# Where the first group's x tiles live, and what the second group's loads wait for, in a hybrid encoder block

## The reference, cut

```
h = rms_norm(x, g_mix); u = h @ w_in + b_in           # GLU value | gate | q | k | v
y_conv = silu(layer_norm(depthwise_conv31(a * sigmoid(gate))))
y_attn = windowed attention (|i-j| <= 128), 8 q heads, 2 kv heads, rotary, sink logit
x += concat(y_conv, y_attn) @ w_out + b_out
x += cross attention (4 heads) from rms_norm(x) into rms_norm(mem), 256 rows
x += (silu(h @ w_gate) * (h @ w_up)) @ w_down         # h = rms_norm(x), width 2816
out = rms_norm(x, g_final)
```

## Time and profile before

| | |
|---|---|
| timed runs | 2018.51 us median of 3 (2016.75 to 2023.31) |
| profiled execution | 2009.25 us, span of its slowest core (2) 2008.0 us |
| spans of the cores | 1985.2 to 2008.0 us |
| mean granted clock | 0.952 to 0.961 |
| busy | PE 1846.9 us (92%), DVE 1109.5 (55%), ACT 873.2 (43%), POOL 120.6 (6%) |
| chain that ended last | PE 78%, DMA 7%, DVE 5%, issue 5%, SP's queue 3%, ACT 2% |

### The profile page before, as it was taken

One profiled execution on the slowest core, in us unless ns is written; L12 is line 12 of the kernel. 1 busy time (PEld: TensorE's weight loads), 2 busy tenths in 40 slices (PEclk: granted clock), 3 DMA queues, 4 the chain that ended last, 5 costly groups with the idle time before them and its releaser, 6 DMA issues.

```text
span 2008.0 us, 34383 instructions; the slowest of 8 cores (1985.2 to 2008.0 us)
## 1 busy us (share of the span) xinstructions
PE 1846.9 (92%) x11516; PEld 974.5 (49%) x11516; DVE 1109.5 (55%) x2430; ACT 873.2 (43%) x1761; POOL 120.6 (6%) x206
## 2 busy tenths in 40 slices
PE   4989998863389999999999999999999999999997
PEld 2545557741135444544454455445444544544443
DVE  5657666553257546643854485467447644754442
ACT  4535534531155444544545354544445453545210
POOL 2100100000100000000000000000001000000000
PEclk7999998766699999999999999999999999999999
DMA  8898865789763316322622363163326223431542
GB/s 263 209 198 217 176 165 168 148 180 194 124 94 127 124 38 235 114 92 79 231 96 93 124 208 116 46 217 119 103 79 219 97 90 132 168 103 56 188 142 100
DMA packets 80934, 284.71 MB, mean 142 GB/s; under 512 B 7159, under 2 KB 38777, under 8 KB 62872
## 3 DMA queue, kind: packets, MB, share of 16 engines
q1 hardware_dynamic: 73592, 237.74, 37.0%
q0 software_dynamic: 2560, 27.99, 10.6%
q10 hardware_dynamic: 4608, 16.78, 2.0%
HBM read 273.16 MB, written 65.10 MB: 168 GB/s over the span
## 4 chain that ended last, share of the span: by engine, by line
PE 78%; DMA 7%; DVE 5%; issue 5%; SPq 3%; ACT 2%; DVEq 0%; ACTq 0%; POOL 0%; POOLq 0%
PE bank L369 52%; PE bank L1447 15%; PE bank L377 5%; DMA arena<-s_y 3%; SPq L359 3%; PE bank L778 2%; PE bank L1086 2%; DMA s_v<-arena 1%; DMA arena<-w_in 1%; PE bank L512 1%; ACT arena L390 1%; PE bank L1090 1%; DVE arena L1368 1%; DVE arena L1056 1%; DVE arena L1211 0%
## 5 line engine op out<-in xcount | busy, mean ns | idle before, releaser
L369 PE MATMUL bank<-arena 128*128 128x512 bf16 (+1 forms) x5724 | 1274.7, 375 | 13.3 <-DVE stat L394 6.6
L369 PEld LDWEIGHTS bank<-arena 128*128 128x128 bf16 x5724 | 555.1, 98 | 616.0 <-issue 38.8
L1447 PE MATMUL bank<-arena 128*128 128x512 bf16 x1408 | 323.2, 379 | 0.6 <-DVE arena L1458 0.6
L390 ACT ACTIVATE arena<-arena 128x1024 bf16<-128x1024 f32 x130 | 137.2, 1055 | 298.5 <-DVE arena L1458 148.6
L377 PE MATMUL bank<-ident,arena 128*128 128x128 bf16 x2080 | 158.1, 224 | 85.3 <-DVE arena L1211 27.2
L1120 ACT ACTIVATE arena<-bank,asm 128x384 bf16<-128x384 f32 (+1 forms) x256 | 146.8, 573 | 145.1 <-DVE asm L1108 128.8
L1447 PEld LDWEIGHTS bank<-arena 128*128 128x128 bf16 x1408 | 133.7, 98 | 149.6 <-issue 7.5
L1413 ACT ACTIVATE arena<-bank 128x512 f32<-128x512 f32 x176 | 105.3, 598 | 229.5 <-PE bank L369 229.0
L377 PEld LDWEIGHTS bank<-ident,arena 128*128 128x128 bf16 x2080 | 137.3, 100 | 130.4 <-issue 98.3
L1104 DVE TENSOR_REDUCE asm<-bank 128x1 f32<-128x384 f32 (+1 forms) x256 | 139.2, 544 | 64.1 <-PE bank L1090 55.0
L1211 DVE TENSOR_TENSOR arena<-bank,arena 128x512 f32<-128x512 f32 x128 | 88.3, 690 | 153.7 <-PE bank L369 122.1
(11 more groups left out here) (85 smaller groups left out, 1292.9 us busy)
## 6 DMA issues: line engine op xcount, KB each, us to landing
arena<-s_gu SPq DMA_DIRECT2D x88, 1024.0 KB, 4.9
arena<-x SPq DMA_DIRECT2D x64, 512.0 KB, 9.2
arena<-s_wd SPq DMA_DIRECT2D x32, 1024.0 KB, 5.0
out<-arena ACTq DMA_DIRECT2D x32, 512.0 KB, 4.0
arena<-s_wd SPq DMA_DIRECT2D x16, 768.0 KB, 4.2
s_gu<-w_gate_up POOLq DMA_DIRECT2D x11, 1024.0 KB, 13.5
s_mem<-w_memory POOLq DMA_DIRECT2D x8, 1024.0 KB, 13.4
arena<-s_mem SPq DMA_DIRECT2D x8, 1024.0 KB, 8.3
```

The source lines that it names most:

```text
L369: ins = nc.tensor.matmul(out_ap, l, r, start=(k == 0), stop=(k == n - 1))
L390: sc.op("act", lambda: nc.scalar.activation(junk, src, AF.Square, accum_out=st[:, 0:1]), reads=[srcb], writes=[junkb, stb], cost=1.26)
L1447: sc.op("pe", lambda t=t, bk=bk: nc.tensor.matmul(bk[:], actT[c][:, t * P:(t + 1) * P], w3[:, c - c0, :], start=(c == 0), stop=(c == NFC - ...
```

## The change

The x tiles of even groups move from 105 to 56 in the arena, those of odd groups from 56 to 105. A list `gate` gets the second matmul group of the output projection of group 0, tile 0. The loads of q, k, v, y and x of group 1 and the first four FFN weight loads wait for it; the y loads of group 1 get 40 us of slack (the first two at once; tiles 2 and 3 are issued by `ln_z` of tiles 0 and 1, as before). The four weight loads waited for the load of `WO` and the last y load of group 0 before. `pace` is called after the projection instead of before it, in `out_proj` and in `s_mm`, so that the cast waits for that projection.

```diff
-    xres = [[mk((105, 56)[s_] + 4 * t, 4, F32, D) for t in range(4)] for s_ in range(2)]
+    xres = [[mk((56, 105)[s_] + 4 * t, 4, F32, D) for t in range(4)] for s_ in range(2)]
...
-            dma("sp", qT.rearrange("p a n -> p (a n)"), s_q[g], [q_g[g]], [qT_b], qT_sem, (), 0.0 if g else 30.0)
+            dma("sp", qT.rearrange("p a n -> p (a n)"), s_q[g], [q_g[g]], [qT_b], qT_sem, gate if g == 1 else (), 0.0 if g else 30.0)
...
+    gate = []
+
     def pace(g):
         if g == 0:
             next_cast([sc.ops[-1]])
...
-        yl_last[0] = dma("sp", ybuf(g, t)[0], s_y[b * P:(b + 1) * P, :], y_b0 + (y_b1 if g else []), [ybuf(g, t)[1]], yt_sem[t % 2 + (2 if g == 0 and t > 1 else 0)])
+        yl_last[0] = dma("sp", ybuf(g, t)[0], s_y[b * P:(b + 1) * P, :], y_b0 + (y_b1 if g else []), [ybuf(g, t)[1]], yt_sem[t % 2 + (2 if g == 0 and t > 1 else 0)], gate if g == 1 else (), 40.0 if g == 1 else 0.0)
...
-                dma("sp", xs[t][0], x_d[b * P:(b + 1) * P, :], [], [xs[t][1]], xres_sem[g % 2][t])
+                dma("sp", xs[t][0], x_d[b * P:(b + 1) * P, :], [], [xs[t][1]], xres_sem[g % 2][t], gate if g == 1 else ())
...
             def a():
+                st["b"] = proj(t, WO, [WO_b], lambda k: ymixT[:, k, t * P:(t + 1) * P], ymc_b + [yma_b[t]], True)
+                if g == 0 and t == 0:
+                    gate.append(sc.ops[-1])
                 pace(g)
-                st["b"] = proj(t, WO, [WO_b], lambda k: ymixT[:, k, t * P:(t + 1) * P], ymc_b + [yma_b[t]], True)
...
             def s_mm():
+                st["s"] = proj(t, WK, WK_b, lambda k: ha[:, k, :], [hb], False)
                 pace(g)
-                st["s"] = proj(t, WK, WK_b, lambda k: ha[:, k, :], [hb], False)
...
     for j in range(NSLOT):
-        ring_load(j, [wo_op, yl_last[0]])
+        ring_load(j, gate)
```

More of the change, by code:

```diff
@@ L965, in f @@
         def f():
-            dma("sp", qT.rearrange("p a n -> p (a n)"), s_q[g], [q_g[g]], [qT_b], qT_sem, (), 0.0 if g else 30.0)
+            dma("sp", qT.rearrange("p a n -> p (a n)"), s_q[g], [q_g[g]], [qT_b], qT_sem, gate if g == 1 else (), 0.0 if g else 30.0)
             gs = sorted(set(b_ // 4 for b_ in range(b0, b1)))
-            dma("sp", kz[:, :, (b0 - lo) * P:(b1 - lo) * P], s_k[:, :, b0 * P:b1 * P], [k_g[k] for k in gs], [kz_b], kz_sem, (), 0.0 if g else 30.0)
-            dma("sp", vz[:, b0 - lo:b1 - lo, :], s_vv[:, b0:b1, :], [vv_g[k] for k in gs], [vz_b], vz_sem, (), 0.0 if g else 30.0)
+            dma("sp", kz[:, :, (b0 - lo) * P:(b1 - lo) * P], s_k[:, :, b0 * P:b1 * P], [k_g[k] for k in gs], [kz_b], kz_sem, gate if g == 1 else (), 0.0 if g else 30.0)
+            dma("sp", vz[:, b0 - lo:b1 - lo, :], s_vv[:, b0:b1, :], [vv_g[k] for k in gs], [vz_b], vz_sem, gate if g == 1 else (), 0.0 if g else 30.0)
             for t in range(2 if g else 4):
```

## The result

The changed kernel takes **2038.49 us** (median of four), the kernel before 2020.91 beside it: a ratio of 1.0085, 95% interval 1.0064 to 1.0105. That is slower by under 1% but clear of the noise, 17.6 us by the medians, where 2016.5 was forecast, and 2.5 us outside the range. One of the four was a slow run, with half of the cores at a lower clock (2320.09 us; the others took 2036.48, 2037.88 and 2039.11), and all ratios, and the medians of the experiments, leave such runs out, while the only profile of the third kernel of number 6 is of one. The profiled execution took 2036.48 us (span of its slowest core, 3: 2035.2 us), 27.2 us more than that of before. It lies 2.0 us under its median, that of before 9.3 us under the median taken with it (2018.51), so the traces show more of a difference than the medians.

What follows compares the result with a forecast made beforehand. TensorE's own work after about 588 us sets the end, so the first group's FFN start counts. Gains -11, -27.1 and -12.3 make -50.4, gated loads give back +48: -2 us, 2016.5 us from 2018.5; 8-in-10 range 1984 to 2036.

Steps and rivals of the forecast that it cites:

- The case forecast: Second group's LayerNorm step ahead of VectorE's last first-group steps, which wait for y: FFN at 593.6, +5.8 us.
- some 9 us to go: VectorE's last first-group steps behind the second group's LayerNorm step, from y's landing to the FFN start: some 9 us.
- G: The gate, end of output projection 0: 485.6 us before, about 474.6 after.
- (b): Second group's first x loads leave SP's queue ahead of the first y loads: y lands 11 us sooner, bounds 0 and 15.5.
- The gated loads: Second group's loads and four FFN weight tiles behind G, among casts: k at G + 71, y at G + 110; +48 us.
- the other order: LayerNorm step behind VectorE's last first-group steps: TensorE waits for k until G + 71; FFN start worth 577.6, -10.2 us.
- (a): First group's x tiles in the region free first: the 27.1 us x wait goes, less what is late next.
- (c): Mixer casts hung on the projection itself, one projection later: taken at 0, between -2 and +3 us.
- The slower rival: Second group's LayerNorm steps and output projections late, first group's FFN covers only part: 2032.5 us, chance 0.20.
- Full and half relief: Full: gated loads in time, 50.4 us stay, 1968 us, chance 0.15; half: two packets for one, 2001.5 us, chance 0.20.
- The middle: FFN start taken between the two places of the LayerNorm step, +5.8 and -10.2: -2 us; forecast's chance 0.45.

Runs made afterwards that it cites:

- the third kernel of number 6: Kernel before with only its nine late casts issued by first-group FFN units 0, 4, 8, 11, 13, 15, 17, 19 and 21: 1978.37 us, ratio 0.9818.
- Experiment 9: Five casts during and after the convolution issued by its first five steps: in the changed kernel 2025.36 us (1.0067), in the best version so far 1972.09 us (0.9799).
- Experiment 7: Changed kernel with 70 instead of 40 us of planner's slack on the second group's first two y loads: 2024.41 us, ratio 1.0045.
- experiment 4: Changed kernel with the second group's x loads free of the gate: a single execution, 2028.7 us.
- the first kernel of experiment 5: Changed kernel with its nine late casts issued by first-group FFN units 0, 2 to 16 instead of the mixers, every gate kept: 2006.99 us, ratio 0.9957.
- experiment 1: Kernel before with only the two x regions exchanged, no gate, casts as before: 2015.11 us, ratio 0.9992.
- experiment 8: Changed kernel with `pace` ahead of the projections again, gates and regions of the change kept: 2033.43 us, ratio 1.0105.

## Why the prediction was wrong

The case forecast is what happened: VectorE reaches the second group's LayerNorm step ahead of its last steps for the first group and waits there until y lands. With that order the prediction had the FFN at 593.6, 5.8 us later than before; it is at 614.0. The 20.4 us between are three terms. The step of the prediction that failed most is the last one, the "some 9 us to go" for the work behind the LayerNorm step: it measured 25.2.

| term | forecast | measured | us |
|---|---|---|---|
| G | 474.6 | 483.6 | +9.0 |
| y of the second group | G + 110 | G + 105 | -4.8 |
| work left behind the LayerNorm step | 9 | 614.0 - 588.8 = 25.2 | +16.2 |

**(b), the first y: mis-sized, and its row half read.** 11 us sooner was forecast. From the end of the convolution to the first LayerNorm step it was 46.4 us before (415.6 to 462.0 on the profiled core) and is 40.6 now, 6 us less; a y load takes 26.1 instead of 33.2 us, 7 less. So 5 of the 9 us are that; 3.5 more are the convolution's own end, 419.1 instead of 415.6, which differs from core to core by more than that (406.8 to 420.4 in the changed kernel). Over the eight cores the median of G is 481.7 against 482.9 before: 1 us sooner where 11 were forecast. The 141 GB/s of the step came from the row of SP's queue in 426 to 462 us. The same answer has a second row, which the prediction left out:

```profile
q0 software_dynamic: 96, 2.10, 49.3%
```

Two casts held half the DMA time there. In the changed kernel they still do (96 packets, 2.10 MB, 49.2%): three x loads fewer do not free that half. Experiment 9 shows it: without the casts the same loads land in 9.7 us. It is the very rule that the prediction printed in bold, applied to the late loads and not to the early ones.

**The work behind the LayerNorm step: the term that cost most.** The 9 us were the distance of the last residuals from the FFN in the kernel before, as if only these stood behind the step. In fact the memory attention of two tiles, their projections and norms did (the chain of waits from 588.8 on: 16 transposes, the copy of L1312, 16 matmuls, the residual, and much of it once more). The size is steady: from the step to the FFN it is 25.2 to 27.9 us on the eight cores. The kernel before had shown that it is no 9: there a LayerNorm step of the second group that waited for y ran at 542.0 and the FFN started 45.8 us behind it. That was its third tile's, not the first, so it gives no more than an upper bound, but it was read and not used. The prediction's own figures say as much: the step at G + 46 in the order and an FFN at G + 62.8 leave 16.8 us behind the step and not 9. Experiment 7 moves the step and takes back 14 us.

**The gated loads: right in the whole, wrong in a part.** y at G + 110 was forecast, it landed at G + 105. k was forecast at G + 71 and landed at 487.6 + 93.8 = 581.4, G + 98. This cost nothing here, since the y wait covers it, and would have cost in the other order (46.6 us in experiment 7). The x loads queued behind k are not the reason: in experiment 4 there are none, and k still takes 93.3 us from issue to landing (14.6 in the first kernel of experiment 5, without casts). Its packets are. The DMA queues of the changed kernel in 521 to 575 us, then those of experiment 4 in 500 to 575:

```profile
q0 software_dynamic: 689, 4.71, 69.4%
q1 hardware_dynamic: 699, 3.04, 27.7%
```

```profile
q0 software_dynamic: 799, 6.58, 72.3%
q1 hardware_dynamic: 801, 3.60, 22.0%
```

The counts are equal, as the forecast took them to be. But it counted all of the 5.1 MB up to k as packets of 8 KB. k is laid out in two runs of 1.5 KB for each of 128 partitions, 256 packets (the first kernel of experiment 5 shows 256 between 0.5 and 2 KB in 485 to 503 us); q, with 4 KB a partition, makes 128. That is 384 turns instead of 112, and with the 362 turns of SP's queue in 550 to 575 us I estimate 272 / 14.5 = 19 of the 27 us from it. Over 521 to 575 us SP's queue thus moved 56 GB/s. That y came at G + 105 all the same is in part luck: by 575 eight of the nine casts were nearly through and the ninth is issued only at 590.2, so that SP's queue then had the engines almost to itself (2.67 MB in 11 us).

**(a) and (c)** held: no wait for x (experiment 1), no cost of the moved `pace` (experiment 8).

**The slower rival** was right in its sign and not in its mechanism. It had the second group's late steps cost time inside the FFN; TensorE is busy 99% from 614 us on. The loss is the forecast's own mechanism with larger terms. **Full and half relief** fell. The 1612 packets beside 736 in 521 to 586 us look like the two for one of the half relief and are not: up to 575 us they are 699 beside 689, and the rest, 913 beside 47, is the end, when the casts have run out.

**The middle was no case.** The forecast of -2 us was the mean of two orders worth +5.8 and -10.2. Given that the chip does one or the other, and that the trace and the prediction's own G + 46 against G + 62.8 put the LayerNorm step ahead of the FFN, the +5.8 should have been taken: 7.8 us of the miss. By the medians the miss is 22 us (2038.5 against 2016.5); by the profiled executions it is 29 us, of which 20.4 and 7.8 are accounted for above.

## What to carry to other kernels

Before loads are reordered around a wait, look at what else is in flight while they move: if another queue's large packets hold the DMA time, the transfer is late wherever it is put, and each wait that is removed comes back at the next load (here x, then y of the second group, then y of the third). Move the bulk copies to a stretch in which nothing is waited for, and spread them there, since in these runs casts close together made loads late just as well 50 us later. And where an in-order engine is to wait, size the cost by all that stands behind the waiting step in its order, for which the trace of before gives an upper bound, the distance from that step to the end of the stage. And a forecast by packet counts needs each load's packet size, not only its bytes.

## What the hardware showed

**Casting copies take nearly all of the DMA time at like packet numbers.** In 489 to 516 us 112 packets of the casts hold 83% of 16 engines' time, 153 packets of SP's queue hold 16% and carry 41 GB/s. A y load of 256 KB takes 9.7 us with no cast in flight, 18.7 to 26.1 with two ahead or beside, and 49.8 behind x loads with the casts of the down weights. The Trainium skill, "DMA: Bandwidth & Descriptors", section Queues, rings and completion order, says that a DMA engine takes turns between the queues, one packet at a time. The trace agrees where both queues have work all the time: 689 beside 699 packets in 521 to 575 us, and 799 beside 801 in experiment 4, while the bytes are 4.71 beside 3.04 MB and 6.58 beside 3.60. The unequal counts of the longer stretches (112 beside 153, 736 beside 1612) hold moments in which only one queue has work.

**Issuing itself can stall.** SP spent 39.5 us on issuing four x loads of 512 KB behind 5.1 MB of queued loads, and 10.9 and 19.2 us on the next two rows. In the first kernel of experiment 5 the same four, behind the same loads but without the casts, took it 4.0 us, so it is not the queued bytes alone but how slowly they drain. The x tiles' place was free by then: in experiment 4 SP had issued them all by 467 us. What stands in SP's program behind such an issue goes out late, whatever it waits for itself; here the casts would have held it anyway (experiment 4).
